# The first rows of the tail block are transposed before the final norm instead of after it

## The chip, the cores and the metric

The kernel runs on one core of a Trainium2 chip. The metric is the device time in microseconds of one execution. Engines are named as in the profile: PE is TensorE, DVE is VectorE, ACT is ScalarE, POOL is GpSimd, SP issues most DMAs. PEld is the load of PE's stationary operand.

## The reference

Two blocks run one behind the other on 256 rows of 1024 numbers. The first is a small diffusion transformer of two layers (mixer, then a mixture of 16 experts), closed by a final norm. The second block (the "tail" here) starts with a parallel mixer. Only the seam between them matters:

```python
def rms_norm(x, g):
    xf = x.astype(jnp.float32)
    y = xf * lax.rsqrt(jnp.mean(xf * xf, axis=-1, keepdims=True) + EPS)
    return (y * g.astype(jnp.float32)).astype(x.dtype)

# end of first_block
        h = h + m[:, :, 5] * ec_moe(...)
    return rms_norm(h, final_g)

# start of second_block
    h = x
    for _ in range(DEPTH_2):
        h = h + parallel_mixer(rms_norm_2(h, norm_mix_g), w_in, ...)
```

Both norms divide each row by a number of its own and multiply each column by a gain. `parallel_mixer` begins with `xn @ w_in`, whose columns are cut into nine parts.

## The kernel before

`h` holds the 256 rows as two tiles of 128 rows (t = 0, 1), 1024 columns each. Each engine has its own written-out program, and semaphores tie them together; the order on an engine is the order in which the code is written. Nothing is planned or reordered. `experts(LOOPS[4])` is the last loop of expert groups; in its last iteration PE makes four products with `sel_w` (line 2227), DVE adds each to a half of `h` (line 1513), and counts `mo_h`. `h` of tile 0 is complete at the second addition, `h` of tile 1 at the fourth.

Then comes the seam.

- DVE forms `rows = h * final_bc` for both tiles (line 1628); `final_bc` is the final gain copied to all partitions.
- PE transposes `rows` by 128x128 pieces into four banks of PSUM (`transposes("mix2", ...)`, line 1883, 16 transposes). The row factor 1/rms of the final norm is left out here and is multiplied in much later, with that of the next norm, as `row_scale`.
- ACT takes `squares("final", ...)` (line 570), a row sum of squares for each tile. POOL makes `rstd` of it in two instructions a tile (lines 1022 and 1023). DVE then writes `h = rows * rstd` (line 1632), the residual that later layers add to, and counts `h_final`.
- Matrix products in the tail run in three passes of a short float format, so each input is split in a high part and the rest. ACT writes the high part of the transposed rows, `norm_high("mix2", rows_hi)` (line 609, eight instructions, two for each bank), and DVE the rest, `norm_low("mix2", rows_hi)` (line 1168, eight). Both multiply by `gcol[:, GAIN["mix2"], :]`, the next norm's gain laid along partitions. `rows_hi` lies in the memory of `rows`, which is why ACT waits for all four banks (`norm_T`) and for `h_final` of both tiles.
- Weights are split likewise, in halves of 128x2048: `high(i)` on ACT (line 600), `low(..., i)` on DVE (line 453). `w_small` holds 48 odd columns, and its rest is line 1636 on DVE. `w_gqk`, `w_fq` and `w_fk` follow.
- PE waits for the two parts of the rows, makes the `w_small` product (24 matmuls, line 1918) and that of `w_gqk` (two halves of 48 matmuls, `split_columns`). It then needs `h_final` to be 3: POOL's `row_scale` (line 1086), which stands behind `squares("mix2", ...)` on the finished `h` and two more POOL instructions a tile. PE broadcasts it (line 2326), DVE copies it, and the gates of the mixer hang on that.

On ACT the order is: both halves of `w_gqk`, squares of the final norm, wait for `h_final`, `norm_high`, squares of "mix2", `w_fq`. On DVE: `rows`, `h`, `w_small`'s rest, `norm_low`, both halves of `w_gqk`, both of `w_fq`.

```python
            high(FIRST["w_gqk"])
            squares("final", h, xT_rows, "mo_h", 8 * GROUPS - 1, 2)
            act.wait_ge(sem("h_final"), 2)
            norm_high("mix2", rows_hi)
            squares("mix2", h, mem_junk, "h_final", 1)
            high(FIRST["w_fq"])
```

Of the kernel before, what the change touches and what calls it, by code (L numbers as in the profile page):

```python
# [9 lines left out]
ALU = mybir.AluOpType  # L10
AX = mybir.AxisListType

P = 128
# [103 lines left out]
def build(nc, a):  # L117
    ctx = ExitStack()
    with ctx:
# [23 lines left out]
        glam = sb("gla_mask", [P, P], I32)  # L143
        gcol = sb("gain_cols", [P, 8 + SCK, KD])
        mcol = sb("mod_cols", [P, 10, KD])
# [223 lines left out]
        NORM_BANKS = {n: (4, 5, 6, 7) for n in TRANSPOSED}  # L369
        NORM_BANKS["moe0"], NORM_BANKS["moe1"] = (4, 5, 2, 3), (0, 1, 2, 3)  # L370
        NORM_BANKS["xattn"] = (1, 2, 6, 7)
        NORM_BANKS["mlp"] = (2, 3, 6, 7)
# [14 lines left out]
        SC_SPLITS = EV_SPLITS + 16  # L387
        GAINS = (6 + SCK) * KD
        NORM2 = 6 + SCK
        cw1 = gcol[:, 6:6 + SCK, :].rearrange("p j c -> p c j")  # L390
# [68 lines left out]
        def _(sp):  # L459
# [37 lines left out]
            for g in (a["norm1_g"], a["norm_mix_g_2"].unsqueeze(0), a["norm_mem_g_2"].unsqueeze(0),  # L497
                      a["norm_xattn_g_2"].unsqueeze(0), a["norm_mlp_g_2"].unsqueeze(0), a["sc_conv_w"][0]):
                n = KD * g.shape[0]
                sp.dma_start(grow[first:first + n, :], g.rearrange("l (k p) -> (l k) p", k=KD)).then_inc(sem("gains_in"), 16)  # L500
                first += n
# [49 lines left out]
        def _(act):  # L551
# [50 lines left out]
            def norm_high(name, dst):  # L602

                v, bank, scale = TRANSPOSED.index(name), NORM_BANKS[name], affine(name)[0]
                for b in range(4):

                    act.wait_ge(sem("norm_T"), 4 * v + (4 if dst is rows_hi else b + 1))
                    for k in (2 * b, 2 * b + 1):
                        last = nc.scalar.activation(dst[:, k, :], ps[:, bank[b], 256 * (k % 2):256 * (k % 2) + 256], ACT.Copy,
                                                    scale=scale[:, k:k + 1])  # L610
                    last.then_inc(sem("x_high"), 1)
# [231 lines left out]
            nc.scalar.activation(small_hi[1], slot8(N0)[:, 5:8, 0:48], ACT.Copy).then_inc(sem("w_high"), 1)  # L843
            high(FIRST["w_gqk"])
            squares("final", h, xT_rows, "mo_h", 8 * GROUPS - 1, 2)
            act.wait_ge(sem("h_final"), 2)
            norm_high("mix2", rows_hi)
            squares("mix2", h, mem_junk, "h_final", 1)
            high(FIRST["w_fq"])
# [285 lines left out]
        def _(dve):  # L1135
# [113 lines left out]
            ada_rows(0, 0)  # L1249
            dve.wait_ge(sem("gain_cols"), 1)  # L1250
            mod_cols(0, 0)
            transposed("x", xT)
# [371 lines left out]

            dve.wait_ge(sem("final_in"), 16)
            u = NORMS.index("final")
            for t in range(NT):
                nc.vector.tensor_tensor(rows[:, t, :], h[:, t, :], final_bc, ALU.mult).then_inc(sem("norm_rows"), 1)
            for t in range(NT):
                dve.wait_ge(sem("norm_rstd"), 2 * u + t + 1)  # L1630
                dve.wait_ge(sem("norm_rows"), 2 * NORMED.index("final") + t + 1)
                nc.vector.tensor_scalar(h[:, t, :], rows[:, t, :], rstd[:, u, t:t + 1], None, ALU.mult).then_inc(sem("h_final"), 1)

            dve.wait_ge(sem("w_high"), SC_SPLITS + 1)
# [3 lines left out]
            last.then_inc(sem("w_split"), 1)  # L1638

            norm_low("mix2", rows_hi)  # L1640
            low(dve, nc.vector, FIRST["w_gqk"])
            low(dve, nc.vector, FIRST["w_fq"])
# [205 lines left out]
        def _(pe):  # L1848
# [24 lines left out]

            def transposes(name, src, ready="norm_rows", first=None):

                v, bank = TRANSPOSED.index(name), NORM_BANKS[name]
                first = 2 * NORMED.index(name) + 1 if first is None else first
                for t in range(NT):
                    if ready:
                        pe.wait_ge(sem(ready), first + t)  # L1880
                    for k in range(KD):
                        cols = run_slice(src[:, t, :], k) if name in ("moe0", "moe1") else src[:, t, P * k:P * (k + 1)]
                        last = nc.tensor.transpose(ps[:, bank[k // 2], 256 * (k % 2) + P * t:256 * (k % 2) + P * (t + 1)],  # L1883
                                                   cols, ident)
                        if t == NT - 1 and k % 2:
                            last.then_inc(sem("norm_T"), 1)
# [88 lines left out]
            for q in range(3):  # L1975
                ada(0, q, 0)
            pe.wait_ge(sem("gains_in"), 7 * 16)
            nc.tensor.transpose(ps[:, 1, 0:GAINS], grow[0:GAINS, :], ident[0:GAINS, 0:GAINS])
# [180 lines left out]
            def experts(loop):  # L2159
                l, g0, g1, base = loop  # L2160
                with pe.Fori(g0, g1) as g:
# [63 lines left out]
                    for i in range(4):  # L2225
                        t, half = i // 2, i % 2
                        mm(pb((6, 7, 4, 5)[i]), sel_w[:, P * t:P * (t + 1)], ym[:, 512 * half:512 * half + 512],
                           start=True, stop=True).then_inc(sem("mo_comb"), 1)
                pe.wait_ge(sem("mo_h"), 4 * (GROUPS * l + g1) + 1)

# [80 lines left out]

            transposes("mix2", rows, first=2 * NORMED.index("final") + 1)
            x = (rows_hi, xT_r)
# [328 lines left out]
```

## Time and profile before

| what | value |
|---|---|
| three runs | 1703.74, 1707.01, 1727.58 us |
| median | 1707.01 us |
| the profiled execution, its own time | 1703.73 us |
| its span, first to last instruction | 1701.9 us |
| PE busy | 1445.8 us, 85% |
| mean granted clock of PE | 0.975 |
| seam: last product of the experts ends, first of the tail starts | 1293.3 us, 1302.5 us |

Times inside the profile are microseconds from the start of the span. 1.8 us lie outside the span. "Idle before" in a row is the time the engine stood still ahead of it, and behind the arrow stands what ended that.

### The profile page before, as it was taken

Reading aid. Unit: us, or ns where it says so; the run is one execution under the profiler, and the core shown is the slowest. Engines: PE = TensorE matmul, PEld = TensorE weight load, DVE = VectorE, ACT = ScalarE, POOL = GpSimd, SP = SyncE. Lnnn points to the kernel's source line nnn. Section 1 sums busy time; section 2 is a strip of 40 time slices with the busy share of each in tenths; the row PEclk is TensorE's granted clock in tenths of the full one; section 3 lists DMA queues with packets and bytes.
Section 4 is the critical chain, followed back from the end, with each engine's and each line's share of the span. In section 5 each row is a group of like instructions: output and inputs, shape, how many; then the busy total and the mean of one; then the engine's idle time right before and its main releaser. Section 6 shows DMA issues by size and latency. Waiting matters only on the chain. (4 is left out here: it accounts for less than half of the span.)

```text
span 1701.9 us, 17970 instructions
## 1 busy us (share of the span) xinstructions
PE 1445.8 (85%) x7722; PEld 786.3 (46%) x7722; DVE 484.8 (28%) x736; ACT 349.6 (21%) x523; POOL 114.4 (7%) x107
## 2 busy tenths in 40 slices
PE   5999978788887898699787877778777999999999
PEld 2744632232231232199421212222115767788997
DVE  1486530100110000166501001001004754435453
ACT  1122420010010000133200100000003634644432
POOL 0000000000000000100000000000003043440000
PEclk9999989999999999999899999999999989999999
DMA  9979969999999999994499999999999523425520
GB/s 374 405 320 413 374 253 422 416 414 421 417 421 422 413 421 421 406 372 166 179 422 421 422 422 422 422 421 422 422 422 355 188 100 130 145 105 193 198 100 25
DMA packets 110000, 561.83 MB, mean 330 GB/s; under 512 B 8516, under 2 KB 9908, under 8 KB 54126
## 3 DMA queue, kind: packets, MB, share of 16 engines
q1 hardware_dynamic: 105880, 551.76, 80.5%
q0 software_dynamic: 2208, 8.36, 1.4%
q8 instruction: 51, 0.84, 0.2%
q10 hardware_dynamic: 1846, 0.75, 0.2%
q14 instruction: 15, 0.12, 0.0%
HBM read 557.69 MB, written 3.16 MB: 330 GB/s over the span
## 5 line engine op out<-in xcount | busy, mean ns | idle before, releaser
L2178 PE MATMUL ps<-ring,scratch 128*32 128x512 f32 x3072 | 613.5, 599 | 138.8 <-DMA ring<-in_moe_w_down 64.0
L2178 PEld LDWEIGHTS ps<-ring,scratch 128*32 128x32 f32 x3072 | 153.7, 110 | 573.5 <-issue 336.5
L1918 PE MATMUL ps<-ring_parts,scratch_parts 128*128 128x512 f32 x656 | 185.8, 401 | 4.9 <-DVE xT_parts L1177 1.4
L1918 PE MATMUL ps<-scratch_parts,ring_parts 128*128 128x256 f32 x704 | 145.5, 282 | 0.0
L1918 PEld LDWEIGHTS ps<-ring_parts,scratch_parts 128*128 128x128 f32 x656 | 121.7, 188 | 35.3 <-issue 3.4
L600 ACT ACTIVATE ring_parts<-ring 128x2048 fp32r<-128x2048 f32 x56 | 106.2, 1918 | 92.2 <-PE ps L1918 86.0
L453 DVE TENSOR_TENSOR ring_parts<-ring,ring_parts 128x2048 fp32r<-128x2048 f32 x46 | 105.3, 2289 | 53.5 <-ACT ring_parts L600 52.2
L1918 PEld LDWEIGHTS ps<-scratch_parts,ring_parts 128*128 128x128 f32 x704 | 115.6, 190 | 0.3
L1507 DVE TENSOR_TENSOR scratch<-ps,gate_bc 128x512 f32<-128x512 f32 x16 | 11.1, 692 | 291.8 <-PE ps L2178 291.8
L1496 DVE TENSOR_TENSOR scratch<-scratch,ps 128x1024 f32<-128x1024 f32 x8 | 9.8, 1222 | 257.0 <-PE ps L2178 257.0
L1918 PE MATMUL ps<-xT_parts,ring_parts 128*128 128x256 f32 x288 | 81.1, 282 | 1.3 <-DVE xT_parts L1168 1.3
L1903 PE MATMUL ps<-ring,xT 128*128 128x512 f32 x160 | 71.2, 605 | 2.6 <-DVE xT L1156 2.6
L736 ACT ACTIVATE scratch<-ps,mod_cols,scale_cols 128x128 f32<-128x128 f32 x32 | 12.9, 453 | 262.7 <-PE ps L2194 262.7
L1918 PE MATMUL ps<-ring_parts,xT_parts 128*128 128x512 f32 x160 | 64.0, 400 | 0.0
L748 ACT ACTIVATE scratch<-ps 128x512 f32<-128x512 f32 x8 | 4.8, 597 | 267.0 <-PE ps L2216 267.0
L1918 PE MATMUL ps<-ring_parts,rows_parts 128*128 128x512 f32 x160 | 55.3, 415 | 0.2 <-DVE ring_parts L453 0.2
L1918 PEld LDWEIGHTS ps<-xT_parts,ring_parts 128*128 128x128 f32 x288 | 54.3, 188 | 1.8 <-issue 1.5
L1863 PE MATMUL ps<-ring,silu_c 128*32 128x512 f32 x384 | 48.0, 634 | 7.7 <-issue 6.8
L2194 PE MATMUL ps<-scratch,rows 128*128 128x128 f32 (+1 forms) x256 | 42.5, 324 | 14.1 <-DVE scratch L1536 5.7
L2194 PEld LDWEIGHTS ps<-scratch,rows 128*128 128x128 f32 x256 | 37.9, 228 | 32.1 <-issue 31.0
L1903 PEld LDWEIGHTS ps<-ring,xT 128*128 128x128 f32 x160 | 30.8, 194 | 40.3 <-issue 37.4
L1492 DVE SCALAR_TENSOR_TENSOR scratch<-ps,cst,scratch 128x256 f32<-128x256 f32 x8 | 3.9, 484 | 159.5 <-ACT scratch L740 159.5
(392 smaller groups left out, 1507.4 us busy)
## 6 DMA issues: line engine op xcount, KB each, us to landing
ring<-in_moe_w_gate SPq DMA_DIRECT2D x64, 2048.0 KB, 30.0
ring<-in_moe_w_up SPq DMA_DIRECT2D x64, 2048.0 KB, 23.1
ring<-in_moe_w_down SPq DMA_DIRECT2D x64, 2048.0 KB, 32.8
ring<-in_ada_w SPq DMA_DIRECT2D x24, 2048.0 KB, 14.5
ring<-in_mlp_w SPq DMA_DIRECT2D x16, 2048.0 KB, 8.8
ring<-in_sc_w_in SPq DMA_DIRECT2D x6, 2048.0 KB, 21.4
ring<-in_w_in SPq DMA_DIRECT2D x6, 2048.0 KB, 18.5
ring<-in_xattn_wkv SPq DMA_DIRECT2D x4, 2048.0 KB, 33.5
```

The lines of the kernel that those rows point to most:

```text
L453: ops.tensor_tensor(lo, w, hi.bitcast(F32), ALU.subtract).then_inc(sem("w_split"), 1)
L600: nc.scalar.activation(hi, w, ACT.Copy).then_inc(sem("w_high"), 1)
L736: last = nc.scalar.activation(xsT[:, k, :], ps[:, GATHER[b], P * (k % 2):P * (k % 2 + 1)], ACT.Identity, scale=scale[:, k:k + 1], bias=shi ...
L748: nc.scalar.activation(flat(hT[:, 4:8, :]), pb(7), ACT.Copy).then_inc(sem("mo_hT_act"), 1)
L1492: nc.vector.scalar_tensor_tensor(sel_w, ps[:, 4, 0:N], cst[:, C_T:C_T + 1], aff_bc, ALU.is_equal, ALU.mult)\
L1496: nc.vector.tensor_tensor(hid, hid, ps[:, 2:4, :].rearrange("p b f -> p (b f)"), ALU.mult)\
L1507: nc.vector.tensor_tensor(ym[:, 512 * j:512 * j + 512], pb(4 + j), gate_bc[:, 512 * j:512 * j + 512], ALU.mult).then_inc(sem("mo_ym"), 1)
L1863: last = mm(ps[32 * j:32 * j + 32, bank, :], lhs, rhs, start=(c == k == 0), stop=(c == 3 and k == 1))
L1903: last = mm(ps[:, banks[t], col:col + width], lhs[:, k, P * t:P * (t + 1)], slot8(i)[:, k, 0:width], start=(k == 0), stop=(k == KD - 1))
L1918: last = mm(out, lhs[x], rhs[y], start=start and n == 0, stop=stop and n == 2)
L2178: last = mm(ps[32 * j:32 * j + 32, banks[half], :], src[:, k, CAP * j:CAP * (j + 1)], w[:, j % (EG // RUN), F * (k % RUN) + col:F * (k % R ...
L2194: last = mm(ps[:, GATHER[b], P * (k % 2):P * (k % 2 + 1)], run_slice(rows[:, t, :], k), onehot[:, t, bass.ds(g * P, P)], start=(t == 0), s ...
```

## The change

The row factor and the column gain of a norm can be applied in either order. The transposes now read `h` itself. The final gain is laid along partitions with the other gains (one more DMA of 4 KB at the start, eight more rows in one small transpose) and multiplied once into the gain of "mix2", 128x8 numbers, at the start of the program. `rows` is not formed any more, so `rows_hi` has no reader to wait for, and ACT goes bank by bank. The squares, the row factor and the residual's update come behind: DVE's two passes over `h` become one instruction a tile (`h * rstd * final_bc`). The halves of `w_gqk` are split one before and one after. The transposes go to banks 0 to 3 instead of 4 to 7, and PE no longer waits at the end of this expert loop for `h` of both tiles.

```diff
         NORM_BANKS["moe0"], NORM_BANKS["moe1"] = (4, 5, 2, 3), (0, 1, 2, 3)
+        NORM_BANKS["mix2"] = (0, 1, 2, 3)
...
-                    act.wait_ge(sem("norm_T"), 4 * v + (4 if dst is rows_hi else b + 1))
+                    act.wait_ge(sem("norm_T"), 4 * v + b + 1)
...
-            high(FIRST["w_gqk"])
-            squares("final", h, xT_rows, "mo_h", 8 * GROUPS - 1, 2)
-            act.wait_ge(sem("h_final"), 2)
+            high(FIRST["w_gqk"], (0,))
             norm_high("mix2", rows_hi)
+            squares("final", h, mem_junk, "mo_h", 8 * GROUPS - 1, 2)
+            high(FIRST["w_gqk"], (1,))
             squares("mix2", h, mem_junk, "h_final", 1)
             high(FIRST["w_fq"])
...
+            nc.vector.tensor_tensor(gcol[:, GAIN["mix2"], :], gcol[:, GAIN["mix2"], :], gcol[:, FINAL_G, :], ALU.mult)
             mod_cols(0, 0)
...
-            dve.wait_ge(sem("final_in"), 16)
-            u = NORMS.index("final")
-            for t in range(NT):
-                nc.vector.tensor_tensor(rows[:, t, :], h[:, t, :], final_bc, ALU.mult).then_inc(sem("norm_rows"), 1)
-            for t in range(NT):
-                dve.wait_ge(sem("norm_rstd"), 2 * u + t + 1)
-                dve.wait_ge(sem("norm_rows"), 2 * NORMED.index("final") + t + 1)
-                nc.vector.tensor_scalar(h[:, t, :], rows[:, t, :], rstd[:, u, t:t + 1], None, ALU.mult).then_inc(sem("h_final"), 1)
-
             dve.wait_ge(sem("w_high"), SC_SPLITS + 1)
...
+            low(dve, nc.vector, FIRST["w_gqk"], (0,))
             norm_low("mix2", rows_hi)
-            low(dve, nc.vector, FIRST["w_gqk"])
+            dve.wait_ge(sem("final_in"), 16)
+            u = NORMS.index("final")
+            for t in range(NT):
+                dve.wait_ge(sem("norm_rstd"), 2 * u + t + 1)
+                nc.vector.scalar_tensor_tensor(h[:, t, :], h[:, t, :], rstd[:, u, t:t + 1], final_bc, ALU.mult, ALU.mult)\
+                    .then_inc(sem("h_final"), 1)
+            low(dve, nc.vector, FIRST["w_gqk"], (1,))
             low(dve, nc.vector, FIRST["w_fq"])
...
-                pe.wait_ge(sem("mo_h"), 4 * (GROUPS * l + g1) + 1)
+                if l == 0:
+                    pe.wait_ge(sem("mo_h"), 4 * g1 + 1)
...
-            transposes("mix2", rows, first=2 * NORMED.index("final") + 1)
+            transposes("mix2", h, "mo_h", 8 * GROUPS - 1, 2)
```

The orders of two engines show the move. DVE before, from the end of the expert loop to the copy of the row factors (`ring_parts_51` is `w_small`'s rest, `_52` that of `w_gqk`, `_53` that of `w_fq`, `xT_parts_57` that of the rows):

```order
266 L1628 TENSOR_TENSOR rows<-h,scratch 128x1024 x2
267 L1632 TENSOR_SCALAR h<-rows,rstd 128x1024 x2
268 L1636 TENSOR_TENSOR ring_parts_51<-ring,ln_row_parts_62 128x5x48
269 L1636 TENSOR_TENSOR ring_parts_51<-ring,silu_c_parts_63 128x3x48
270 L1168 SCALAR_TENSOR_TENSOR xT_parts_57<-ps,gain_cols,rows_parts_58 128x256 x8
271 L453 TENSOR_TENSOR ring_parts_52<-ring,ring_parts_49 128x8x256 x2
272 L453 TENSOR_TENSOR ring_parts_53<-ring,ring_parts_50 128x2048 x2
273 L1647 COPY gate_bc<-ps 128x256
```

DVE now, the same stretch:

```order
267 L1631 TENSOR_TENSOR ring_parts_51<-ring,ln_row_parts_62 128x5x48
268 L1631 TENSOR_TENSOR ring_parts_51<-ring,silu_c_parts_63 128x3x48
269 L455 TENSOR_TENSOR ring_parts_52<-ring,ring_parts_49 128x8x256
270 L1171 SCALAR_TENSOR_TENSOR xT_parts_57<-ps,gain_cols,rows_parts_58 128x256 x8
271 L1641 SCALAR_TENSOR_TENSOR h<-h,rstd,scratch 128x1024 x2
272 L455 TENSOR_TENSOR ring_parts_52<-ring,ring_parts_49 128x8x256
273 L455 TENSOR_TENSOR ring_parts_53<-ring,ring_parts_50 128x2048 x2
274 L1649 COPY gate_bc<-ps 128x256
```

One split of a weight half now stands ahead of the rows' rest, and the residual's update behind it, ahead of the second half. ACT before, the same stretch:

```order
150 L600 ACTIVATE ring_parts_49<-ring 128x2048 x2
151 L570 ACTIVATE xT,ss<-h 128x1024 x2
152 L609 ACTIVATE rows_parts_58<-ps,gain_cols 128x256 x8
153 L570 ACTIVATE scratch,ss<-h 128x1024 x2
154 L600 ACTIVATE ring_parts_50<-ring 128x2048 x2
155 L852 ACT_TABLE_LOAD
```

ACT now:

```order
150 L603 ACTIVATE ring_parts_49<-ring 128x2048
151 L612 ACTIVATE rows_parts_58<-ps,gain_cols 128x256 x8
152 L573 ACTIVATE scratch,ss<-h 128x1024 x2
153 L603 ACTIVATE ring_parts_49<-ring 128x2048
154 L573 ACTIVATE scratch,ss<-h 128x1024 x2
155 L603 ACTIVATE ring_parts_50<-ring 128x2048 x2
156 L855 ACT_TABLE_LOAD
```

The rows' high part moved ahead of one weight half and of the squares of the final norm. On PE and POOL the instructions stand as they stood; only the source of PE's 16 transposes changed, from `rows` to `h`.

## Rows read from the trace of the kernel before

**Rows 1.** The page: its first line.

```profile
span 1701.9 us, 17970 instructions
```

**Rows 2.** Timeline of PE at the seam: start, duration, line, idle before.

```profile
1289.57 3.70 PE L2227 MATMUL ps<-scratch 128*128 128x512 f32 x8 [0.79 <-DVE scratch L1507]
1295.40 2.14 PE L1883 MATMUL ps<-cst,rows 128*128 128x128 f32 x16 [2.13 <-DVE rows L1628]
1302.46 0.42 PE L1918 MATMUL ps<-xT_parts,ln_row_parts 128*48 128x256 f32 x1 [4.93 <-DVE xT_parts L1168]
...
1307.59 0.42 PE L1918 MATMUL ps<-xT_parts,ring_parts 128*128 128x256 f32 x1
...
1319.27 0.61 PE L2326 MATMUL ps<-cst,ms 128*128 128x128 f32 x4
```

**Rows 3.** Timeline of DVE at the seam.

```profile
1293.30 0.69 DVE L1513 TENSOR_TENSOR h<-h,ps 128x512 f32<-128x512 f32 x1 [0.17 <-PE ps L2227]
1294.03 2.36 DVE L1628 TENSOR_TENSOR rows<-h,scratch 128x1024 f32<-128x1024 f32 x2
...
1299.78 0.75 DVE L1632 TENSOR_SCALAR h<-rows,rstd 128x1024 f32<-128x1024 f32 x1 [0.71 <-POOL rstd L1023]
1300.45 0.40 DVE L1636 TENSOR_TENSOR ring_parts<-ring,ln_row_parts 128x240 fp32r<-128x240 f32 x1
...
1301.44 3.23 DVE L1168 SCALAR_TENSOR_TENSOR xT_parts<-ps,gain_cols,rows_parts 128x256 fp32r<-128x256 f32 x8 [0.37 <-ACT rows_parts L609]
1304.58 9.47 DVE L453 TENSOR_TENSOR ring_parts<-ring,ring_parts 128x2048 fp32r<-128x2048 f32 x4
```

**Rows 4.** Timeline of ACT at the seam.

```profile
1292.61 3.71 ACT L600 ACTIVATE ring_parts<-ring 128x2048 fp32r<-128x2048 f32 x2 [6.12 <-DMA ring<-in_w_in]
1296.23 1.04 ACT L570 ACTIVATE xT<-h 128x1024 f32<-128x1024 f32 x1
...
1300.57 3.02 ACT L609 ACTIVATE rows_parts<-ps,gain_cols 128x256 fp32r<-128x256 f32 x8 [2.17 <-DVE h L1632]
...
1305.51 3.76 ACT L600 ACTIVATE ring_parts<-ring 128x2048 fp32r<-128x2048 f32 x2
```

**Rows 5.** Timeline of POOL at the seam.

```profile
1297.46 0.19 POOL L1022 TENSOR_SCALAR ms<-ss 128x1 f32<-128x1 f32 x1 [3.39 <-ACT xT L570]
...
1304.73 2.19 POOL L1022 TENSOR_SCALAR ms<-ss 128x1 f32<-128x1 f32 x1 [4.10 <-ACT scratch L570]
1307.00 2.69 POOL L1023 TENSOR_TENSOR rstd<-ms,mhalf 128x1 f32<-128x1 f32 x1
...
1314.54 0.19 POOL L1086 TENSOR_TENSOR ms<-rstd 128x2 f32<-128x2 f32 x1
```

**Rows 6.** Windows at the seam: stretch, length, busy times, PE's clock, DMA share.

```profile
1301.00:1302.00 1.00, 0.00 (x0) 0.00 (x0) 0.63 (x3) 1.00 (x4) 0.00 (x0) 0.57 1.05 387
1302.00:1307.00 5.00, 4.54 (x22) 4.23 (x23) 4.89 (x9) 5.00 (x10) 2.19 (x2) 0.50 1.05 383
1307.00:1308.00 1.00, 1.00 (x6) 0.97 (x5) 1.00 (x1) 1.00 (x2) 1.00 (x1) 0.51 1.06 389
```

**Rows 7.** Timeline of PE at two other stops of like length.

```profile
570.16 2.30 PE L2178 MATMUL ps<-ring,scratch 128*32 128x512 f32 x6 [2.77 <-DMA ring<-in_moe_w_down]
...
616.21 2.00 PE L2194 MATMUL ps<-scratch,rows 128*128 128x128 f32 x15 [2.64 <-ACT xT L784]
```

**Rows 8.** Windows behind those stops, and in a later stretch.

```profile
571.00:573.00 2.00, 2.00 (x6) 0.37 (x4) 0.00 (x0) 0.00 (x0) 0.00 (x0) 0.50 0.99 388
...
618.00:620.00 2.00, 2.00 (x11) 0.63 (x12) 0.15 (x1) 0.81 (x2) 0.00 (x0) 1.00 1.03 422
...
1377.00:1389.00 12.00, 12.00 (x40) 6.67 (x39) 5.01 (x4) 1.28 (x8) 6.64 (x2) 0.50 0.21 77
```

**Rows 9.** Timeline of DVE at the program's start.

```profile
32.32 0.17 DVE L1198 COPY mod_cols<-ps 128x8 f32<-128x8 f32 x1 [0.82 <-PE ps L1871]
```

**Rows 10.** PE's waits from 1303 us to the end: total, times, longest.

```profile
PE ps L1918 <- DVE xT_parts L1168: 2.5, 2, 1.3
```

More of the change, by code:

```diff
@@ L143, in build @@
         glam = sb("gla_mask", [P, P], I32)
-        gcol = sb("gain_cols", [P, 8 + SCK, KD])
+        gcol = sb("gain_cols", [P, 9 + SCK, KD])
         mcol = sb("mod_cols", [P, 10, KD])
@@ L387, in build @@
         SC_SPLITS = EV_SPLITS + 16
-        GAINS = (6 + SCK) * KD
-        NORM2 = 6 + SCK
+        FINAL_G = 6 + SCK
+        GAINS = (7 + SCK) * KD
+        NORM2 = 7 + SCK
         cw1 = gcol[:, 6:6 + SCK, :].rearrange("p j c -> p c j")
@@ L497, in _ @@
             for g in (a["norm1_g"], a["norm_mix_g_2"].unsqueeze(0), a["norm_mem_g_2"].unsqueeze(0),
-                      a["norm_xattn_g_2"].unsqueeze(0), a["norm_mlp_g_2"].unsqueeze(0), a["sc_conv_w"][0]):
+                      a["norm_xattn_g_2"].unsqueeze(0), a["norm_mlp_g_2"].unsqueeze(0), a["sc_conv_w"][0],
+                      a["final_g"].unsqueeze(0)):
                 n = KD * g.shape[0]
@@ L1872, in ada_columns, with transposes @@
                 last.then_inc(sem("mod_T"), 1)
-            def transposes(name, src, ready="norm_rows", first=None):
+            def transposes(name, src, ready="norm_rows", first=None, step=1):
                 v, bank = TRANSPOSED.index(name), NORM_BANKS[name]
@@ L1879, in transposes @@
                     if ready:
-                        pe.wait_ge(sem(ready), first + t)
+                        pe.wait_ge(sem(ready), first + step * t)
                     for k in range(KD):
@@ L1976, in _ @@
                 ada(0, q, 0)
-            pe.wait_ge(sem("gains_in"), 7 * 16)
+            pe.wait_ge(sem("gains_in"), 8 * 16)
             nc.tensor.transpose(ps[:, 1, 0:GAINS], grow[0:GAINS, :], ident[0:GAINS, 0:GAINS])
```

## Prediction

> **What bounds the kernel now.** The profiled execution took 1703.73 us around a span of 1701.9 [rows 1]. I went from the page straight to PE's timeline at the seam, because the change touches nothing else of weight. The reader should see one hole there: the last product of the experts ends at 1289.57 + 3.70 = 1293.27, the transposes run from 1295.40 to 1297.54, and the first product of the tail starts at 1302.46 [rows 2]. PE stands still for 2.13 and 4.93 us. From then on it has work all the way to 1319.27 [rows 2]. Behind 1303 us no stop of PE is put down to a DMA, and the longest total is 2.5 us [rows 10]. So the tail is a chain of PE work, and what is saved in the hole should reach the end.
>
> The timelines of DVE, ACT and POOL say what fills the hole. PE's first wait is for `rows` on DVE, which starts at 1294.03 [rows 3]. The second is a long way round: ACT splits two halves of `w_gqk` from 1292.61, comes to the squares at 1296.23 [rows 4], POOL takes 1297.46 and on [rows 5], DVE finishes `h` of tile 1 at 1299.78 + 0.75 = 1300.53 [rows 3], ACT starts the high parts at 1300.57 [rows 4], DVE the rest at 1301.44 [rows 3]. PE starts 1.02 later, that is two of the eight instructions (3.23 / 8 = 0.40 each, 0.81 a pair) and 0.21 for the signal.
>
> The clock is the second cost. PE's granted clock is 0.57 in the microsecond from 1301, so it fell from 2.4 to 1.2 GHz at about 1301.1; it is 0.50 to 1307 and 0.51 in the microsecond from 1307, so it came back at about 1308.0 [rows 6]. Before the fall PE had stood still for 3.6 us. The 24 matmuls of `w_small` run from 1302.46 to 1307.59 [rows 2], 0.214 each, where 0.107 would be full speed. The low clock lay over 1308.0 - 1302.5 = 5.5 us of work and cost half, 2.75 us.
>
> **The change, part by part.**
>
> The start of the program. One more multiplication of 128x8 numbers on DVE, about 0.17 us by its neighbour, goes in where DVE waits 0.82 us for PE [rows 9]. Hidden. The extra DMA of 4 KB is one more small issue ahead of large loads; I take 0 of it, and 0.3 us as the other end.
>
> Transposes. Tile 0 of `h` is complete before PE is through with its last product at 1293.27, so its eight transposes (2.14 / 16 = 0.134 each [rows 2]) run to 1294.3. Tile 1 is complete at 1293.30 + 0.69 = 1293.99 [rows 3], earlier than PE gets there. All 16 end at about 1295.4, against 1297.54. The first bank is whole at 1293.27 + 10 x 0.134 = 1294.6.
>
> ACT. The first half of `w_gqk` still waits for its DMA and runs from 1292.61 to 1292.61 + 3.71 / 2 = 1294.5 [rows 4]. `norm_high` then needs the first bank and a signal: 1294.8, and with 3.02 for the eight [rows 4] it ends at 1297.8.
>
> DVE. It is free at 1293.99. `w_small`'s rest takes 0.7 (0.40 [rows 3] and a smaller one), to 1294.7. Now comes the half of `w_gqk` that the change puts in front: its high part is ready at the same moment, and it takes 9.47 / 4 = 2.37 [rows 3], to 1297.0. This is the new last link, longer than ACT's: the first pair of `norm_low` would be possible at 1295.8 and starts at 1297.0, so the chosen order leaves 1.2 us lying. Then 0.81 and 0.21: **PE starts the tail at 1298.0**, not at 1302.46. That is 4.4 us.
>
> The clock. PE's stop is now 1295.4 to 1298.0, 2.6 us instead of 4.93. Two other stops of that length stand in the trace, 2.77 us before 570.16 and 2.64 us before 616.21 [rows 7]. Behind the first the clock was 0.50 in the window from 571 to 573, behind the second it was 1.00 [rows 8]. So a stop of this length may or may not cost a low stretch. PE's work from its start to the row factors is 24 x 0.107 = 2.6 and 1319.27 - 1307.59 = 11.7 us [rows 2], 14.3 at full speed. At full speed the first product is paced by DVE instead, 3 x 0.81 + 0.64 = 3.1, half a microsecond more than 2.6. A shorter low stretch than before, some 3.4 us (half of the 6.8 seen), costs 1.7. With it PE comes to the row factors at 1298.0 + 14.3 + 1.7 + 0.1 = 1314.1, against 1319.27: **5.2 us earlier**. With no low stretch it is 1298.0 + 14.3 + 0.5 = 1312.8, 6.5 us. With one as long as before, over 6.8 us of work, 1298.0 + 14.3 + 3.4 = 1315.7, 3.6 us.
>
> What is late next. The squares (two of 1.04 and a short reading each, 2.2 together) run on ACT from 1297.8 to 1300.0, the second half of `w_gqk` to 1302.0. POOL has the factors at about 1299.9 and 1301.0 by its short row of 0.19 [rows 5]. DVE ends `norm_low` at 1297.0 + 3.2 = 1300.2 and writes `h`, two instructions over 128x1024 with two inputs, 2.36 / 2 = 1.18 each by the row that read as much [rows 3]: 1302.6 to 1303.4. The second half's rest follows, to 1305.8 at the latest. PE asks for it at 1298.0 + 3.1 + 5.8 = 1306.9 at the earliest. Hidden by 1.1 us or more. The second squares run as soon as `h` is written, to 1304.6, and POOL needs 1314.54 + 0.19 - 1304.73 = 10.0 us behind the first of them as before [rows 5], that is from 1303.4 to 1313.4 at most. PE asks at 1312.8 to 1315.7. In the fastest case that costs 0.6 to 0.8 us, in the likeliest nothing. The rest of `w_fq` on DVE ends at about 1311. Hidden.
>
> POOL's own price hangs on DVE. An instruction of 128x1 took 0.19 us at 1297.46 and 2.19 us at 1304.73, where DVE had begun a 2.37 us instruction at 1304.58 and ended it as POOL did [rows 3, 5]. The Trainium skill, SBUF — State Buffer, section "Who interferes with whom", says that a DVE instruction with two SBUF inputs contends with a GpSimd instruction that reads SBUF. By that, the trace agrees, and the new update of `h`, which reads two, can hold POOL as well.
>
> **The sum.** 1703.73 - 5.2 = 1698.5 us for an execution like the profiled one. Two of the four executions shown stand at 1703.7, the median is 1707.01; 1707.0 - 5.2 would be 1701.8. I put the forecast between, at **1700.0 us**.
>
> **The rivals.**
>
> *No low clock at all.* For it speaks the stop before 616.21. PE arrives 6.5 us earlier and waits some 0.7 for POOL's row factors: 5.8 to 6.5, 1697.2 to 1697.9.
>
> *The clock falls as long as before.* The edge at 1301.1 does not care that PE has work again, or the first product is too thin to bring the clock back. 3.6 us, 1700.1.
>
> *The gain is given back later.* The clock is low without a stop of PE for 12 us from 1377 [rows 8]; all work there shifts by 5 us, and that stretch or another can come out 3.4 us longer or shorter, 1.7 us either way. With one longer the gain is 3.5 us, with two 1.8: 1700.2 to 1701.9.
>
> *Slower.* One mechanism: DVE holds POOL in the norm that now runs behind. If all four POOL instructions of the final norm take their long durations, 2 x (2.19 + 2.69) = 9.8 us from 1299.0, the second `h` is written at 1310.0, the second half of `w_gqk` at 1312.4, PE ends it at 1318.2, the second squares end at 1311.4 and POOL's 10.0 us bring the row factors at 1321.4, 2.1 us behind 1319.27: 1705.9. It decides from the point where tile 1's factor comes 6 us or more after 1301. Against it speaks that DVE waits for just these factors from 1300.2 on, and a waiting DVE holds nothing.
>
> *The change does not do what it says.* The orders show that it does; the one weak place is ACT's wait for the DMA of `w_gqk` at 1292.6 [rows 4]. If that lands x later, the tail starts x later in both kernels, so the difference stays.
>
> **How the numbers follow.** Short low clock 0.40, none 0.22, long 0.15, given back later 0.15, slower 0.05, something else 0.03. For the range I take the low end from no low clock and one low stretch less later, 1703.7 - 6.5 - 1.7 = 1695.5, rounded down to 1695, and the high end from the slower case on the median's level, 1707.0 + 2.1 = 1709. A measurement of this kernel can tell about 2%, 34 us, and no case comes near it: faster 0.01, within 0.98, slower 0.01.
>
> **What would show it.** PE's transposes start at 1293.3 with no idle time and end at 1295.4; the first product of the tail starts at 1298.0, released by line 1171 on DVE; ACT's high parts start at 1294.8; the `h` update of tile 1 ends by 1303.4; the row factors' broadcast starts at about 1314 with no idle time. I would be wrong if the update of `h` ended after 1306, if the stop of PE were as long as before, if the broadcast waited for POOL by more than a microsecond, or if PE stood still later for longer than it did.

## The result and the profile after

The changed kernel is slower: a median of 1724.74 us over 20 runs (1702.18 to 1726.95) against 1705.65 us over 20 runs of the kernel before (1703.12 to 1728.85). The ratio on record is 1.0076, with a 95% interval of 1.0053 to 1.0100: within 2%, and clear of the noise. (The medians alone stand in the ratio 1.0112; where runs lie at two levels, the number depends on how it is formed.) The forecast was 1700.0 and the range ended at 1709.

The median hides the shape. The changed kernel's times lie at two levels with nothing between: six at 1702.2 to 1704.8, fourteen at 1724.0 to 1727.0. The kernel before has the same two levels, eighteen at 1703.1 to 1709.3 and two at 1727.6 and 1728.9. At its lower level the change gains about 2 us; what it did was to move most runs to the upper one. PE's mean granted clock tells the levels apart in every run of the changed kernel: 0.969 to 0.974 in the six, 0.952 to 0.960 in the fourteen.

The profiled execution took 1704.76 us, so its trace is of the lower level. The page's first line, beside [rows 1]:

```profile
span 1702.9 us, 17967 instructions
```

PE at the seam, in the timeline of the changed kernel (start, duration, line, idle before), to be read beside [rows 2]:

```profile
1292.03 3.70 PE L2229 MATMUL ps<-scratch 128*128 128x512 f32 x8 [0.80 <-DVE scratch L1511]
1295.57 2.04 PE L1885 MATMUL ps<-cst,h 128*128 128x128 f32 x16
...
1300.45 0.29 PE L1920 MATMUL ps<-xT_parts,ln_row_parts 128*48 128x256 f32 x1 [2.85 <-DVE xT_parts L1171]
...
1316.31 0.60 PE L2329 MATMUL ps<-cst,ms 128*128 128x128 f32 x4
```

The experts end at 1295.73 here and at 1293.27 before, 2.46 us later. What lies ahead of the seam scatters (in the fourteen traces of this document the experts end anywhere from 1292.1 to 1297.9, with either kernel), so the seam is read from that end. The transposes start with no idle time. The tail's first product starts 4.72 us behind the experts' end, where it was 9.19. The row factors' broadcast starts 20.58 us behind it, where it was 26.00. The seam is 5.4 us shorter.

DVE at the seam, beside [rows 3]:

```profile
1295.77 0.69 DVE L1517 TENSOR_TENSOR h<-h,ps 128x512 f32<-128x512 f32 x1 [0.17 <-PE ps L2229]
...
1297.22 2.29 DVE L455 TENSOR_TENSOR ring_parts<-ring,ring_parts 128x2048 fp32r<-128x2048 f32 x1
1299.43 3.22 DVE L1171 SCALAR_TENSOR_TENSOR xT_parts<-ps,gain_cols,rows_parts 128x256 fp32r<-128x256 f32 x8
1302.57 2.47 DVE L1641 SCALAR_TENSOR_TENSOR h<-h,rstd,scratch 128x1024 f32<-128x1024 f32 x2
1304.96 2.28 DVE L455 TENSOR_TENSOR ring_parts<-ring,ring_parts 128x2048 fp32r<-128x2048 f32 x1
```

DVE works through without a wait: the weight half, the rows' rest, both updates of `h`, the second half. ACT, beside [rows 4]:

```profile
1295.07 1.91 ACT L603 ACTIVATE ring_parts<-ring 128x2048 fp32r<-128x2048 f32 x1 [6.11 <-DMA ring<-in_w_in]
1296.99 3.02 ACT L612 ACTIVATE rows_parts<-ps,gain_cols 128x256 fp32r<-128x256 f32 x8
```

POOL in the second norm, beside [rows 5]:

```profile
1305.12 2.16 POOL L1025 TENSOR_SCALAR ms<-ss 128x1 f32<-128x1 f32 x1 [1.59 <-ACT scratch L573]
1307.37 0.56 POOL L1026 TENSOR_TENSOR rstd<-ms,mhalf 128x1 f32<-128x1 f32 x1
1308.02 0.19 POOL L1025 TENSOR_SCALAR ms<-ss 128x1 f32<-128x1 f32 x1
1308.29 2.46 POOL L1026 TENSOR_TENSOR rstd<-ms,mhalf 128x1 f32<-128x1 f32 x1
1310.84 1.97 POOL L1089 TENSOR_TENSOR ms<-rstd 128x2 f32<-128x2 f32 x1
```

POOL is done at 1312.8, 3.5 us before PE asks. DVE pauses between 1307.24 and 1308.06. The first of the two quick rows in the middle lies in that pause and the second begins as it ends; each slow one ends within 0.4 us of the end of a DVE instruction with two SBUF inputs (line 455). A busy DVE alone does not make POOL slow: the two short POOL instructions of the final norm's first tile, at 1301.14 and 1301.41, took 0.19 and 0.56 us while DVE was at line 1171, which reads one of its two large inputs from PSUM.

So the seam did what it was meant to do, and the loss is behind it. From the broadcast's start to the end of the span it is 1702.9 - 1316.3 = 386.6 us, against 1701.9 - 1319.3 = 382.6 before, though no instruction there was edited. Windows of the two traces, first the changed kernel, then the kernel before (stretch, length, busy times of PE, PEld, DVE, ACT, POOL, then PE's clock, the DMA share and GB/s):

```profile
1370.00:1380.00 10.00, 10.00 (x38) 5.77 (x36) 4.96 (x5) 3.79 (x4) 6.55 (x2) 0.62 0.61 211
1380.00:1390.00 10.00, 10.00 (x34) 6.38 (x33) 2.95 (x3) 1.28 (x8) 5.39 (x4) 0.50 0.00 0
1390.00:1400.00 10.00, 10.00 (x46) 7.64 (x46) 0.76 (x2) 1.28 (x8) 5.44 (x6) 0.86 0.00 0
1410.00:1430.00 20.00, 19.76 (x105) 14.47 (x105) 11.91 (x30) 10.90 (x30) 9.11 (x2) 1.00 0.01 2
```

```profile
1370.00:1380.00 10.00, 9.92 (x44) 6.43 (x42) 7.30 (x12) 5.01 (x6) 5.26 (x2) 0.81 0.60 211
1380.00:1390.00 10.00, 10.00 (x33) 6.04 (x32) 2.95 (x3) 1.28 (x8) 4.64 (x3) 0.51 0.00 0
1390.00:1400.00 10.00, 10.00 (x54) 7.75 (x53) 0.76 (x2) 1.28 (x8) 7.54 (x8) 1.00 0.00 0
```

PE is busy in both, but more of it is at 1.2 GHz: the low stretch lasts from 1372.4 to 1392.9, 20.5 us, where it was 13.65, from 1376.2 to 1389.9. At half speed that is up to 3.4 us lost of the 5.4 gained. Another 0.94 us is lost in the last products of the program; the section on e2_start_only shows where it comes from. What the upper level is, this trace cannot show.

### The profile page after: what moved, and what is told of

The parts are those of the page before. It is cut to its first block and busy times, and to the rows that moved or that the text cites. A ratio compares the mean times of both kernels' runs of the same rounds, so it can differ in the third digit from the quotient of the medians.

```text
span 1702.9 us, 17967 instructions
## 1 busy us (share of the span) xinstructions
PE 1453.0 (85%) x7722; PEld 791.2 (46%) x7722; DVE 482.8 (28%) x735; ACT 349.8 (21%) x523; POOL 111.3 (7%) x107
```

## The experiments

Each experiment ran in up to twelve executions, in three groups on three chips (e1 to e4, e5 to e8, e9 to e12), with the kernel before between them: its medians were 1704.95 (30 runs, two above 1715), 1705.77 (31 runs, two) and 1704.96 (23 runs, none). "Upper" counts runs above 1715 us. "Seam" is from the experts' end to the row factors' broadcast and "rest" from there to the end of the span, both in the profiled execution.

| kernel | upper | median | seam | rest |
|---|---|---|---|---|
| before | 2 of 20 | 1705.65 | 26.0 | 382.6 |
| after | 14 of 20 | 1724.74 | 20.6 | 386.6 |
| e1_again (after) | 7 of 12 | 1720.13 | 20.4 | 408.9 |
| e2_start_only | 0 of 11 | 1704.59 | 25.8 | 383.6 |
| e3_after_wait | 4 of 12 | 1706.56 | 24.8 | 385.6 |
| e4_before_wait | 5 of 6 | 1730.61 | 26.9 | 408.0 |
| e5_after_fill | 0 of 11 | 1703.65 | 20.6 | 385.2 |
| e6_before_fill | 0 of 11 | 1705.99 | 25.3 | 384.5 |
| e7_after_wait_2 | 3 of 8 | 1702.93 | 22.6 | 383.7 |
| e8_before_wait_3 | 1 of 12 | 1709.12 | 29.6 | 382.6 |
| e9_after_fill_wait | 0 of 12 | 1702.33 | 22.5 | 383.8 |
| e10_after_fill_full | 0 of 6 | 1694.58 | 20.5 | 378.6 |
| e11_before_fill_full | 0 of 12 | 1699.93 | 25.8 | 377.2 |
| e12_rows_first | 0 of 6 | 1695.24 | 19.5 | 378.6 |

### Where the 22 us are: e1_again

The changed kernel with no edit.

> The changed kernel once more, for a trace at its upper level. Its 20 times lie at two levels, 1702 to 1705 (6) and 1724 to 1727 us (14), those of before at 1703 to 1709 (18) and 1727 to 1729 (2). Mean clock is 0.957 at the upper level and 0.970 at the lower, and (0.043 x 1724 - 0.030 x 1701) = 23 us is the whole distance. Theory A (one long low clock in the tail): a trace at the upper level agrees with the one at hand up to the seam and has some 45 us more of low clock in one stretch behind it, most likely grown out of the stretch from 1372 to 1393. Theory B (many places): the low clock is spread over the whole program. Theory C (the start): the first 120 us are longer.

Measured: 1720.13 us median, ratio 1.0044 (1.0004 to 1.0084), seven of twelve runs at 1719 to 1727. The profiled execution took 1725.29, so this is a trace of the upper level. Its windows and its timeline of PE in the attention of the mixer ("fox" in the code), where small products alternate with blocks of `w_out`:

```profile
1399.00:1400.90 1.90, 1.90 (x15) 1.44 (x14) 0.13 (x1) 0.76 (x2) 0.71 (x1) 1.00 0.17 11
1400.90:1404.20 3.30, 2.01 (x9) 1.22 (x8) 2.74 (x8) 2.47 (x7) 0.00 (x0) 1.00 0.93 328
1404.30:1410.00 5.70, 5.70 (x18) 4.23 (x17) 1.84 (x7) 1.27 (x5) 0.00 (x0) 0.50 0.44 168
1410.00:1430.00 20.00, 20.00 (x60) 14.02 (x58) 7.44 (x21) 6.58 (x19) 4.53 (x1) 0.50 0.00 1
1430.00:1451.00 21.00, 21.00 (x65) 15.66 (x65) 5.66 (x13) 5.96 (x14) 4.54 (x1) 0.50 0.00 0
1452.00:1460.00 8.00, 8.00 (x37) 6.50 (x36) 2.13 (x4) 1.43 (x3) 1.17 (x2) 1.00 0.58 221
```

```profile
1400.47 0.49 PE L2448 MATMUL ps<-scratch 64*128 64x128 f32 x4
1402.12 0.97 PE L1920 MATMUL ps<-ring_parts,scratch_parts 128*128 128x512 f32 x3 [1.15 <-DVE scratch_parts L1180]
1403.22 0.33 PE L2456 MATMUL ps<-cst,scratch 128*128 128x128 f32 x1
```

Read the last column but two. The clock is 1.00 until 1404.2 and 0.50 from there to 1452.0, 47.8 us on end, while PE is busy all the time by its records. The same 20 us window holds 60 products here and 105 in the trace of the lower level above. Nearly all of the distance is in this one stretch: the rest is 408.9 us, 22.3 more than in the other trace of the same program. Of that, 1.6 are there when PE restarts at 1402.12 (87.6 us behind the broadcast, against 86.0), because the low stretch around 1375 is 23.9 us long and not 20.5; the other 20.8 come behind it. Theory A holds, with the place one stretch further on than I had guessed; B and C fall. What stands ahead of the fall is a stop of 1.15 us, in which PE waits for DVE's part of the first `w_out` input; PE restarts 2.1 us before the fall. The stop alone is not enough: it stands at 1402.35 in the trace of the lower level too, as long, and there the clock does not fall.

### Not the start: e2_start_only

```diff
-            nc.vector.tensor_tensor(gcol[:, GAIN["mix2"], :], gcol[:, GAIN["mix2"], :], gcol[:, FINAL_G, :], ALU.mult)
+            nc.vector.tensor_tensor(gcol[:, FINAL_G, :], gcol[:, GAIN["mix2"], :], gcol[:, FINAL_G, :], ALU.mult)
```

This line of the change, its DMA and its transpose, all in the kernel before; nothing else of the change.

> The kernel before with the change's part at the start alone: one more DMA of 4 KB, 80 instead of 72 rows in a transpose, one more DVE multiplication of 128x8 numbers (its result is used by nobody). The seam is as before. Theories A and B: as before, 1703 to 1709 us in nearly all runs, ratio 1.000 within 0.003. Theory C: the upper level (1724 to 1727) in about 7 runs of 10.

Measured: 1704.06 to 1706.85, median 1704.59, ratio 1.0001 (0.9992 to 1.0010). The start brings no upper level, and what it costs is less than these times can tell, since 0.1% is 1.7 us. The traces can tell it. The last piece of the chain that ends last is 1152 products at the end of the program (start, duration, what), first the kernel before, then this run:

```profile
1517.56 180.39 PE ps L1918 x1152
```

```profile
1516.93 181.33 PE ps L1921 x1152
```

The same 1152 products take 180.38 or 180.39 us in all five traces without the change's part at the start (before, e4, e6, e8, e11) and 181.33 to 181.35 in all nine with it. So this part costs 0.94 us, from 200 us behind the seam on, in products that it does not touch. Besides the DMA and the multiplication it makes one buffer, `gain_cols`, longer by eight numbers a partition. Which of these does it was not tested.

### What a shift alone does: e3, e4, e7 and e8

All four add constant transposes on PE ahead of the row factors' broadcast: 40 and 19 to the changed kernel, 11 and 31 to the kernel before.

```diff
+            for _ in range(11):
+                nc.tensor.transpose(ps[:, 3, 0:P], ident, ident)
             pe.wait_ge(sem("h_final"), 3)
```

> The changed kernel with 40 more transposes of a constant on PE just ahead of the row factors' broadcast, 0.134 us each by the transposes' row, or 0.06 if they run back to back at full rate: 2.4 to 5.4 us that push all that follows back to about where it lay before. Theory A in the form that the shift of the tail's work against the clock's edges decides: fewer runs at the upper level, about 1 in 10 if the delay is near 5.4, and the lower level at 1704 to 1708. If the level hangs on what the seam itself does to the clock: still 7 in 10 at the upper level, at 1727 to 1732.

> The kernel before with 11 of the same transposes at the same place, 0.7 to 1.5 us. The shift form of theory A: the share of the upper level moves away from 1 in 10, since 5.4 us earlier and 1.4 us later differ by 6.8 us, the length of two of the shortest low stretches seen (3.41), so that clock edges fall on the same work; 7 in 10 at 1725 to 1731. If the shift does not matter: 1 in 10, lower level at 1704 to 1710.

> The changed kernel with 19 transposes ahead of the row factors' broadcast (0.109 us each by e3_after_wait, 2.07 us). The tail then lies 5.4 - 2.1 = 3.3 us earlier than before, one of the shortest low stretches seen. Theory A in its shift form (what decides is how the stops fall against the clock's instants, and moves by 3.4 us are the same as none): upper level rare as before (1 in 12), low stretch around 1376 13.65 us long, and the lower level at 1705.0 - 3.3 = 1701.7, although work was added. Rival E (an earlier tail is prone to the upper level as such): half of the runs or more at 1722 to 1727.

> The kernel before with 31 transposes at the same place, 3.4 us. Shift form: as before, upper level rare, lower level at 1708.3, where 11 transposes (1.2 us) put 5 runs of 6 at 1730. Rival F (any delay there brings the upper level): 8 in 10 at 1731 or more.

The transposes took 0.11 us each, so 40 are about 4.4 us and 11 about 1.2. The sharpest result is e4: the kernel before, with 1.2 us of idle work and nothing of the change, has five of six runs at 1730 to 1732 and a ratio of 1.0129 (1.0091 to 1.0167). Its trace has the clock low for 47.8 us from 1411.0, again about 2.2 us behind PE's restart at 1408.8. With 3.4 us in the same place (e8) only one run of twelve is upper, and the median is 1709.12, within a microsecond of the 1708.3 expected: it has more delay than e4 and a lower time. So a later tail is neither good nor bad in itself. That what decides is how it falls against the instants at which the clock changes fits both, and is not shown by itself.

The rule that I had made of it for e7, that such a move is the same as none, is only half right. e7 kept the lower level to the tenth (its five lower runs have a median of 1701.6, expected 1701.7; the low stretch around 1375 is 13.65 us long), but three of eight runs are upper where one in twelve was expected. e3 has four of twelve where one in ten was expected if the delay undid the shift, and seven in ten if it did not matter; it stands between, and twelve runs do not decide. Rival E, that an earlier tail is prone as such, asked for half of e7's runs or more, which three of eight does not rule out; but e4 shows that a later tail can be prone as well. So the share of upper runs is not explained by the size of the shift alone.

One more number comes out of the traces side by side. From the end of the low stretch around 1375 to PE's restart in the attention it is 8.1 us in the two upper traces (1394.0 to 1402.1 in e1, 1400.8 to 1408.8 in e4), and 9.5 to 12.6 us in the six lower ones without a fill (9.5 after, 9.8 e3, 12.3 to 12.6 in before, e2, e7 and e8). The low stretch is 23.9 us long in the two upper traces and 13.65 to 20.5 in the nine others that have one. So the two places may hang together: where the first stretch ends says how the next stop lies to the clock's instants. That is read off eight traces and was not tested by itself.

### Filling the stop: e5 and e6

```diff
                 if n == 0:
+                    for _ in range(5):
+                        mm(pb(FTB[0]), rows_hi[:, 0, 0:P], rows_hi[:, 0:2, :].rearrange("p k n -> p (k n)"), start=True, stop=True)
                     pe.wait_ge(sem("x_split"), 4 * SPLIT_INPUTS.index("w_out") + 2)
```

> The changed kernel with five products of 128x512 (about 0.23 us each) whose result nobody reads, in the 1.15 us in which PE stands still at the first block of the fox attention, 1400.96 to 1402.12 in the trace of e1_again. There the clock fell 2.12 us after PE went on and stayed low for 47.79 us. Theory A (the stop tips the clock, and the thin products behind it keep it down): no run at the upper level, all at 1701 to 1704 us, median about 1702.5. Rival D (the stop is not the trigger; the thin products of 64 rows or 64 columns would tip it anyway): 6 to 7 runs of 10 stay at 1720 to 1727.

> The kernel before with the same five products at the same place. Theory A: no upper level either, median 1704.5 to 1705.5; the rare 1724 to 1729 (4 of 50 so far) gone. Beside e5_after_fill it gives what the change is worth with the fox attention's clock out of play: if all of the 5.4 us that the seam was shortened by arrive, 1699.5 against 1705; if a part is lost in the low stretch around 1370 to 1394 (20.5 to 23.9 us long in the changed kernel, 13.65 before), 1702 against 1705. Rival D: unchanged, 1704.9, now and then 1727.

PE's timeline in e5_after_fill at the place of the stop:

```profile
1400.11 1.43 PE L2482 MATMUL ps<-rows_parts 128*128 128x512 f32 x5
1401.37 0.92 PE L1920 MATMUL ps<-ring_parts,scratch_parts 128*128 128x512 f32 x3
```

The five products nobody reads leave no idle time, and the upper level is gone: 1701.88 to 1706.02 in eleven runs, median 1703.65, ratio 0.9989 (0.9980 to 0.9997). That is 21 us less than the changed kernel's median, by added work. Rival D falls: the thin products behind the stop do not bring the clock down by themselves. The changed kernel without an edit did not run on this chip; the nearest that did is e7, with three upper runs of eight, and at that share eleven runs without one have a chance of under 1%. e6 has no upper run either, at 1705.99, which says little, since two of 31 are upper without the fill. Between e5 and e6 stand 2.3 us, not 5.4.

### Both: e9_after_fill_wait

The edits of e5 and e7 together.

> The changed kernel with both the five products in the fox attention's stop and the 19 transposes ahead of the row factors' broadcast (2.07 us). e5_after_fill alone gave 1703.65, e7_after_wait_2 1700.3 to 1703.5 in its lower runs and three runs at 1726 to 1729. Theory A: no upper level, and as the low stretch around 1375 was 13.65 us long in e7 where it was 17 to 24 in the others, the median is 1701.7 although 2 us of work are added. Rival G (the length of that stretch does not follow from the shift): 1703.65 + 2.1 = 1705.7.

Measured: 1700.82 to 1706.46, median 1702.33, ratio 0.9982 (0.9973 to 0.9992), no upper run (on this chip the kernel before had none in 23 runs, so here that adds little). The low stretch is 13.65 us long in its trace and in e7's, 17.1 in e5's. The median is 0.6 us off the 1701.7 of theory A and 3.4 off rival G. It is 1.3 below that of e5, but on another chip, and the scatter of the two sets of runs is as large; in the traces seam and rest together are 406.3 us against e5's 405.8. So the 2.07 us of added work are mostly made good by the shorter low stretch; that they bring a gain is not shown.

### The low stretch around 1375: e10 and e11

The eight products of the code are 16 instructions in the trace.

```diff
-                    last = mm(ps[:, b, N * w:N * (w + 1)], ident[0:FOXH, hd:hd + 1].broadcast_to([FOXH, P]), lf2[0:FOXH, :],
+                    last = mm(ps[:, b, N * w:N * (w + 1)], ident[:, hd:hd + 1].broadcast_to([P, P]), lf2,
                               start=True, stop=True)
...
+            link(nc.vector.memset(lf2, 0.0))
```

> e5_after_fill, and the eight products that spread the forget gates over the partitions (line 2392 before) read all 128 rows instead of 8; one DVE memset of 128x256 makes the added rows zero. They take as long as before and give the same numbers. The clock fell inside these products at 1372.4 (after), 1370.1 (e1), 1376.2 (before), though PE's records show it busy without a stop. Theory H (PE at work on 8 of 128 rows does not count as at work for the clock): the low stretch of 14 to 24 us starts later, or is shorter or gone; each 3.41 us less of it gives 1.7 us, so 1697 to 1702 against 1703.65. Rival I (it is the products of 64x64 ahead or behind, or time itself): the stretch stays, 1703.7 to 1704.2.

> The same two edits (five products in the stop, 128 rows) on the kernel before, as the partner of e10. If the clock's low stretches in the tail are out of play, e10 stands 5.4 us below this one, which is what the seam was shortened by; if H fails, the distance is that of e5 and e6, 2.3 us.

The clock did not always fall inside these products, as the expectation says: in the kernel before they end at 1376.12 and it fell at 1376.24. In the eleven traces with 8 rows it fell 2.4 to 4.7 us behind the start of the first of them, in five inside them and in six up to 1.0 us behind. The edited products in the timeline of PE, first the kernel before, then e10_after_fill_full (behind the tiles stand PE's rows and columns in use):

```profile
1372.43 3.69 PE L2392 MATMUL ps<-ln_row,cst 8*128 8x256 f32 x16
```

```profile
1367.91 3.72 PE L2396 MATMUL ps<-ln_row,cst 128*128 128x256 f32 x16
```

They take the same time, and PE's busy time does not tell them apart. The clock does. Windows of e10_after_fill_full:

```profile
1370.00:1380.00 10.00, 10.00 (x59) 6.21 (x57) 6.94 (x7) 3.50 (x11) 7.58 (x3) 1.00 0.49 185
1380.00:1390.00 10.00, 10.00 (x55) 7.87 (x52) 0.99 (x3) 1.28 (x8) 9.33 (x9) 1.00 0.00 0
```

The low stretch is gone, in e11 and e12 as well: from the broadcast to the end of the span the three traces stand at 1.00, where all eleven with 8 rows have a stretch of 13.65 to 23.9 us. e10 takes 1694.58 (1693.52 to 1696.18), ratio 0.9939 (0.9924 to 0.9953), and e11 1699.93, ratio 0.9972 (0.9963 to 0.9981). The rests are 378.6 and 377.2 us, 6.6 and 7.3 below those of e5 and e6, whose low stretches of 17.1 us are worth at most half of that, 8.5 (e6's trace, of its slowest run, has a further short one of 3.4 behind the broadcast). Theory H holds in what it says of the stretch; its range of 1697 to 1702 was missed by 2.4 us, on the low side. Whether the clock goes by rows in use or by something that comes with them is not told apart.

1699.93 - 1694.58 = 5.35 us is now the distance between the two kernels, known to about 1.3 us by the scatter of six and twelve runs. That it equals the 5.4 us of the seam is in part luck. Between the two traces the seam is 5.37 us shorter, the rest 1.35 longer (0.95 of that in the 1152 last products), and the experts end 1.49 earlier, which is scatter. So the seam's gain reaches the end but for about a microsecond.

### The order on DVE: e12_rows_first

```diff
-            low(dve, nc.vector, FIRST["w_gqk"], (0,))
             norm_low("mix2", rows_hi)
+            low(dve, nc.vector, FIRST["w_gqk"], (0,))
```

> e10_after_fill_full with DVE's order changed: the rest of the rows ahead of the first half of w_gqk, not behind it. The prediction said that the order leaves 1.2 us lying. In the trace of after ACT ends the half only at 1296.99, so the rows' high part starts there; the first pair of the rest is then possible at about 1298.6 instead of 1300.2, PE starts the tail 1.6 us earlier, and PE asks for w_gqk's first half 3 us later, when DVE has it (2.3 + 3.2 us behind 1297.9 = 1303.4, against 1298.8 + 3.1 = 1301.9: up to 1.5 us of it lost again). Expected gain against e10: 0 to 1.6 us at the seam, within the scatter in the whole.

Measured: 1695.24 (1693.56 to 1696.13), ratio 0.9940 (0.9926 to 0.9955). The seam is 19.50 us, 0.97 shorter than e10's. PE's stop is short, and the clock did not fall there in this trace. PE starts the tail 3.18 us behind the experts' end, 1.53 earlier than in e10, and then waits for the half of `w_gqk` that now comes second on DVE, as the expectation warned:

```profile
1298.49 0.29 PE L1921 MATMUL ps<-xT_parts,ln_row_parts 128*48 128x256 f32 x1 [1.30 <-DVE xT_parts L1171]
...
1302.94 0.38 PE L1921 MATMUL ps<-xT_parts,ring_parts 128*128 128x256 f32 x1 [1.29 <-DVE ring_parts L455]
```

How much of the 0.97 is the order and how much the missing low stretch is not told apart. In the whole it is not distinguished from e10 (six runs each, 2.6 us of scatter).

## Why the prediction was wrong

Going by its own steps:

- **The start, hidden.** Right at the start, wrong in the whole. I put this term at 0, or 0.3 at most; it costs 0.94 us, in the last 1152 products of the program, as the traces show. No upper run comes of it.
- **PE starts the tail at 1298.0,** that is 4.73 us behind the experts' end. Measured 4.72. The last link was the weight half on DVE, as worked out. With the order turned round, in e12, PE starts 1.53 us earlier, where 1.2 were said to be left lying, and waits 1.29 later.
- **The clock at the seam.** A shorter low stretch of 3.4 us was taken as the likeliest, and it was 3.41 us (1300.70 to 1304.11), as in all seven traces of the changed kernel with this order on DVE. The sum for the seam, 5.2 us, was measured as 5.4.
- **What is late next: nothing.** Right. POOL had its factors 3.5 us early; the second half of `w_gqk` was ready at 1307.24, and PE came to it at about 1310.5, half of `w_gqk`'s 11.7 us ahead of the broadcast.
- **"What is saved in the hole should reach the end."** This is the step that failed. It rested on the absence of DMA waits behind 1303 us [rows 10]. That says that no transfer holds PE, but PE's work there has two prices, one at 2.4 and one at 1.2 GHz, and which one it pays differs between runs of the same program. An edit that only moves the tail can change that, as e4_before_wait shows with 1.2 us of work and 25 us of time.
- **The rival "given back later"** named the mechanism and mis-sized it. I priced it at 1.7 us for each low stretch that comes out one step longer, from the stretch at 1377 [rows 8]. In the attention behind it a stretch of 47.8 us appears, at half speed worth up to 24; 20.8 were measured behind the restart, 22.3 with what the stretch ahead of it adds. The size stood in front of me: one of the three times shown was 1727.58, and I treated it as scatter around a median, when 20 to 24 us above three runs that agree within 4 is a second state of the program that wants a cause. Its price and its share of runs should have made the upper end of the range.
- **The levels of the runs.** Putting the forecast between 1698.5 and 1701.8 was too low even for the lower level, 1702.2 to 1704.8. The stretch around 1375 takes most of that, beside the 0.94 us of the last products: it is 17.1 to 23.9 us long in the three traces of the changed kernel without added transposes, 13.65 in that of the kernel before (and 17.1 in e6_before_fill, 23.9 in e4_before_wait, so the length varies there too).

So the change is good for 5.4 us where it acts. In this kernel 2 to 2.5 of them arrive at the lower level, and 21 of 32 runs pay 22 us in a place that the change does not touch. With the stop filled and the eight products on all rows it is worth 5.35 us by the medians and about 4 by seam and rest of the traces, and the kernel stands at 1694.58 us, 0.6% below the kernel before.

Four things stay open. What in the change's part at the start slows the last 1152 products by 0.94 us was not tried. Whether the products on 128 rows would remove the upper level without the fill was not tried. Why a shift of a microsecond changes the share of upper runs, and not only which runs they are, is not settled: the first fall of the clock lies anywhere from 32.8 to 36.2 us in fourteen traces, so its instants are not tied to the program's start, and that the low stretch around 1375 has to do with it is only argued above. And e7's three upper runs don't fit the simple rule of shifts.

## What to carry to other kernels

When the runs of one program lie at two levels, find out which stretch makes the upper one before costing any edit ahead of it, since an edit that only shifts the work behind it can trade one level for the other, and a median of few runs then says nothing of the edit. Judge a local gain by a local distance (here from the experts' end to the broadcast), and check separately that the clock behind it is the same, and that stretches which the edit does not touch take as long as before; here one took 0.94 us more. Where PE's clock falls in front of work that is too thin to bring it back, useless wide products in a stop of one microsecond, or the same product written over all rows, can be worth more than the edit itself.

## What the runs showed of the hardware

- PE's granted clock fell in or just behind 16 products that read 8 of 128 rows (3.7 us, busy by the records), 2.4 to 4.7 us behind the first, in all eleven traces that have them. The same products reading 128 rows take 3.72 us and leave the clock at 1.00, in three traces with different shifts (e10, e11, e12). PE's busy time alone is not what keeps the clock up. The Trainium skill, TensorE: Matmul & The Clock Gate, section "What's actually happening", says that the clock is set by how busy PE has been; by the busy time of the records, 3.69 us with 8 rows and 3.72 with 128, these two would be alike, and the granted clock is not.
- Once at 1.2 GHz, PE stayed there for 47.8 us of work without a stop, in e1 and in e4 alike, through products of 64 rows or 64 columns alternating with blocks of 128x512. In the twelve other traces the same work runs at 2.4 GHz from end to end. In both e1 and e4 a stop of 1.15 us stood ahead, and the clock fell 2.1 to 2.2 us behind its end. The same stop stands in the six lower traces without a fill, and the clock did not fall there. With the stop filled none of 23 runs of the changed kernel (e5, e9) has the time of the upper level.
- A GpSimd instruction on one column takes 0.19 or 2.16 us in the same stretch of the same trace: 2.16 beside a DVE instruction with two inputs in SBUF, 0.19 as DVE's pause ends, and 0.19 beside a DVE instruction that reads one of its two large inputs from PSUM.
- A part of the program that only adds one small DMA, eight rows to a transpose, a multiplication of 128x8 numbers and a longer buffer at the start made 1152 products at the end slower by 0.94 us, 180.39 to 181.33, in nine traces against five. Why stays open.
